# A state space step whose heads, convolution ends and gated norm run as one stream beside the projections

## The chip, the cores and the metric

The kernel runs on one core of a Trainium2 chip. The metric is the device time of one launch in microseconds (us). Before the change the median of 3 runs is 1757.48 us (1754.95 to 1759.02).

## What is computed

Two blocks, one after the other, on 272 rows (16 meta tokens and a sequence of 256) of width 1024, all in float32. The first block is a two-layer model of feed-forward nets, a short convolution and an attention. The second is one mixer layer and a gated convolutional feed-forward net. The change is in the mixer, cut here to what it touches:

```
z, xbc, dt_raw, q, k, v, g_ssd, g_att = split_cols(u @ w_in, IN_WIDTHS)
xbc = silu(causal_dwconv(xbc, conv_w, conv_b))            # 4 taps
xs, bm, cm = split_cols(xbc, (2048, 512, 512))
dt = softplus(dt_raw + dt_bias);  a = -exp(a_log)         # 32 heads of 64
# per head h of group g (8 heads in a group), over chunks of the sequence
cs = cumsum(dt * a)
y  = (C_g B_g^T * exp(cs_t - cs_s), t >= s) @ (x * dt)    # ssd_chunked
y  = y + d_skip * x
g  = y * silu(z)                                          # gated norm
gg = g * rsqrt(mean(g * g over 512 channels) + EPS) * w
merged = sigmoid(g_ssd) * (gg @ w_ssd_branch) + sigmoid(g_att) * (att @ w_attn_branch)
```

The kernel takes the 272 positions at once, in three pieces of 128, 128 and 16, so a head's matrix exp(cs_t - cs_s) is held as 272 + 144 + 16 columns; the last piece (16 rows by 16 columns) is called the corner below.

## The kernel before

**Weights.** Every projection is a sum of products of float32 numbers split in two parts. A weight unit of 1 MB is loaded by SP into one of `raw` buffers (2048 columns, handled in four pieces of 512). ACT writes the high part `wh` of a piece (L1137), then DVE, or POOL for the pieces that the plan names, the low part `wl` (L1626, L1947), and TensorE (PE) takes three products: `XH,wh` and `XL,wh` (L803) and `XH,wl` (L805). With K = 1024 a group of 256 output channels is one unit and 48 matmuls, 24 into each of two PSUM banks; dt, with 32 channels, is 24 matmuls into one. There are `NR` = 4 buffers `raw`, and `NH` = 3 each of `wh` and `wl`; SP loads unit n + 4 once the low part of unit n is written.

**Side steps.** Everything that is no projection is written as a generator on each engine (`pe_steps`, `act_steps`, `dve_steps`, `pool_steps`). All four have the same steps in the same order, some of them empty. A planner (`P`) puts a slot for a step between the matmuls of the groups: `P.rate` is a measure of work per slot, `P.queue(n)` lets n more steps go, `P.credit` holds them back at first, and `P.drain(name)` puts all that are queued before the next group. A step stands at the same slot on every engine, and an engine runs its own instructions strictly in order.

**The mixer's order** is: kv2, q2_0 to 3, z_0 to 7, ga, ya (with the attention's steps beside them), dt, bc_0 to 3 (channels of B and C), xs_0 to 7 (256 channels of x, four heads, each), gs_0 to 3, ys (the branch out of the gated norm).

**Steps of the state space part.** Behind dt come softplus, cumulative sum (DVE, `CSB`, L1415), its transposes (PE L703) and high and low parts `CSH`, `CSL`. `conv4` takes each bc or xs group: a bias and scale out of PSUM on ACT (L1191), three taps for two blocks on DVE (L1684), tanh on ACT (L1197) and its product on DVE (L1689), which ends in `BC` or in one of two buffers `CY`. Four `CB` steps (PE L712, DVE `CBM` L1562) give the products of B and C. For each block c of 128 channels (heads 2c and 2c + 1) there is a T step (PE transposes x, L727; DVE multiplies by dt, `XDT`, L1575), two E steps (PE spreads cs over the partitions, L738; DVE subtracts, L1587, L1588 and for the corner L1590; ACT takes the exponential `EX`; POOL multiplies by `CBM`, L1911, and the corner, L1912) and a y step (PE L643 to L645 into one half of bank 7 for each head; DVE adds the skip into `YB`, L1617; POOL multiplies by silu(z), L1939). The four steps of the gated norm, one for each 512 channels, stand behind all that, beside gs: square on ACT (L1097), sum with a matrix of means on PE (L752), rstd with ln and exp on ACT (L923, L925), product on DVE (L1602), high and low parts `YH` (L1111) and `YL` (L1608).

**The skip's constants.** POOL issues the three small loads `DTB`, `AN`, `DC2` behind ya. Far ahead of them, behind the norm that precedes kv2, it issues the attention's four `B<-strips` loads.

## Time and profile before

| | |
|---|---|
| median of 3 runs | 1757.48 us |
| the profiled execution | 1753.09 us, span 1751.3 us |
| PE busy | 1667.7 us (95%) |
| DVE, ACT, POOL busy | 59%, 52%, 12% |
| mean granted clock of TensorE | 0.986 of 2.4 GHz |
| chain that ended last | PE 84%, issue 4%, ACT 4%, DVE 3%, POOL 3% |
| HBM | 262.89 MB read, 151 GB/s over the span |

The profile is of one execution. Its matmuls are the program's records; a matmul busy for 0.29 us overlaps its neighbour, so the step from one start to the next (about 0.12 us for 258 or 272 columns) is what a matmul takes of the time. "x2" in a row means two records that the view has put together.

### The profile page before, as it was taken

The numbers are of one execution on the slowest core, as the hardware profiler recorded it, in microseconds if no ns is written. First come the engines' busy times: TensorE is split into PE (matmuls) and PEld (weight loads), VectorE is DVE, ScalarE is ACT, GpSimd is POOL, SyncE is SP. The second block draws the span as 40 slices with busy tenths as digits, with TensorE's granted clock in tenths as the row PEclk, the third lists the DMA queues.
The fourth block names the chain that finished last, engine by engine and source line by source line (L and its number), as shares of the span: only waits on it lengthen the run. The fifth ranks groups of instructions, "written<-read, shape, count | busy, mean of one in ns | idle before, by whom it ended". The sixth has DMA issues, their size and how long they took to land.

```text
span 1751.3 us, 31633 instructions
## 1 busy us (share of the span) xinstructions
PE 1667.7 (95%) x12915; PEld 1596.3 (91%) x12915; DVE 1033.4 (59%) x2139; ACT 911.5 (52%) x2008; POOL 217.5 (12%) x257
## 2 busy tenths in 40 slices
...
GB/s 276 175 169 175 182 125 172 122 190 169 177 178 131 169 179 180 194 131 114 121 144 190 177 187 120 176 113 104 113 154 60 78 69 136 201 145 177 179 181 43
DMA packets 260207, 266.00 MB, mean 152 GB/s; under 512 B 4755, under 2 KB 259025, under 8 KB 260064
## 3 DMA queue, kind: packets, MB, share of 16 engines
...
q0 software_dynamic: 1536, 3.28, 0.8%
...
HBM read 262.89 MB, written 1.09 MB: 151 GB/s over the span
## 4 chain that ended last, share of the span: by engine, by line
PE 84%; issue 4%; ACT 4%; DVE 3%; POOL 3%; DMA 0%; SPq 0%; DVEq 0%; POOLq 0%; ACTq 0%
PE ps L803 51%; PE ps L805 25%; POOL EX L1911 2%; PE ps L516 1%; ACT wh L1137 1%; PE ps L772 1%; POOL YB L1939 1%; PE ps L615 1%; POOL EX L1912 0%; ACT H L918 0%; DVE BC L1684 0%; DVE wl L1626 0%; POOL wl L1947 0%; ACT XH L913 0%; PE ps L752 0%
## 5 line engine op out<-in xcount | busy, mean ns | idle before, releaser
L1626 DVE TENSOR_TENSOR wl<-raw,wh 128x512 fp32r<-128x512 f32 x923 | 609.9, 713 | 395.2 <-ACT wh L1137 386.7
L1137 ACT ACTIVATE wh<-raw 128x512 fp32r<-128x512 f32 (+1 forms) x989 | 548.2, 620 | 213.7 <-PE ps L803 212.9
L803 PE MATMUL ps<-XH,wh 128*128 128x272 f32 (+2 forms) x2264 | 577.5, 291 | 16.0 <-ACT XH L913 6.7
L805 PE MATMUL ps<-XH,wl 128*128 128x272 f32 (+2 forms) x2264 | 568.9, 287 | 0.0
L803 PEld LDWEIGHTS ps<-XH,wh 128*128 128x128 f32 x2264 | 431.2, 190 | 21.6 <-issue 14.7
L805 PEld LDWEIGHTS ps<-XH,wl 128*128 128x128 f32 x2264 | 432.5, 191 | 0.2
L803 PE MATMUL ps<-XL,wh 128*128 128x272 f32 (+2 forms) x2264 | 310.6, 288 | 0.2 <-DVE XL L1407 0.2
L803 PEld LDWEIGHTS ps<-XL,wh 128*128 128x128 f32 x2264 | 290.0, 189 | 4.2 <-DVE XL L1407 2.8
L803 PE MATMUL ps<-HH,wh 128*128 128x272 f32 (+1 forms) x704 | 173.1, 284 | 0.0
L805 PE MATMUL ps<-HH,wl 128*128 128x272 f32 (+1 forms) x704 | 173.1, 284 | 0.0
L803 PEld LDWEIGHTS ps<-HH,wh 128*128 128x128 f32 x704 | 132.5, 188 | 0.0
L805 PEld LDWEIGHTS ps<-HH,wl 128*128 128x128 f32 x704 | 132.4, 188 | 0.0
L803 PE MATMUL ps<-KXH,wh 128*128 128x256 f32 (+1 forms) x480 | 121.2, 291 | 2.3 <-ACT KXH L913 2.3
L805 PE MATMUL ps<-KXH,wl 128*128 128x256 f32 (+1 forms) x480 | 118.0, 284 | 0.0
L1947 POOL TENSOR_TENSOR wl<-raw,wh 128x512 fp32r<-128x512 f32 (+1 forms) x66 | 88.1, 1339 | 178.2 <-ACT wh L1137 178.1
L1177 ACT ACTIVATE HH<-SG 128x272 fp32r<-128x272 f32 (+1 forms) x88 | 33.7, 425 | 146.9 <-DVE SG L1643 146.9
L803 PEld LDWEIGHTS ps<-KXH,wh 128*128 128x128 f32 x480 | 91.3, 190 | 7.0 <-issue 5.4
L803 PE MATMUL ps<-HL,wh 128*128 128x272 f32 (+1 forms) x704 | 93.6, 284 | 0.0
L805 PEld LDWEIGHTS ps<-KXH,wl 128*128 128x128 f32 x480 | 91.5, 191 | 0.1
L803 PEld LDWEIGHTS ps<-HL,wh 128*128 128x128 f32 x704 | 89.0, 188 | 0.0
L1172 ACT ACTIVATE SG<-ps 128x272 f32<-128x272 f32 (+1 forms) x88 | 29.6, 388 | 104.8 <-PE ps L803 104.7
L1643 DVE SCALAR_TENSOR_TENSOR SG<-SG,ps 128x272 f32<-128x272 f32 (+1 forms) x88 | 33.8, 425 | 80.0 <-PE ps L803 80.0
...
## 6 DMA issues: line engine op xcount, KB each, us to landing
...
```

The costliest lines, as they stand in the source:

```text
L516: e.matmul(var, mean1[:], SQ[:, k % 4, n0:T], start=k == 0, stop=k == 7).then_inc(s_var, 1)
L615: e.matmul(oo[:, 0:T], VN[:, 0, gs], sw.PT0[:], start=True, stop=False)
L772: mm = e.matmul(PS[6][:, 0:T - n0], mean1[:], SQ2[:, k % 4, 0:T - n0], start=k == 0, stop=k == KD - 1)
L803: mm = e.matmul(o, hi[:, k, c], xk, start=u.first and part == 0 and k == 0, stop=u.last and end)
L805: e.matmul(o, lo[:, k, c], xk, start=False, stop=False)
L1137: e.activation(wh[u.n % NH][:, c], raw[u.n % NR][:, c], ACT.Copy).then_inc(s_hi, 1)
L1172: e.activation(sg[:, m, n0:T], PS[G.b0 + m][:, 0:T - n0], ACT.Silu).then_inc(s_sg, 1)
L1177: e.activation(HH[f][:, 2 * j + m, n0:T], sg[:, m, n0:T], ACT.Copy).then_inc(s_hh, 1)
L1626: e.tensor_tensor(wl[u.n % NH][:, c], raw[u.n % NR][:, c], wh[u.n % NH][:, c].bitcast(F32), ALU.subtract).then_inc(s_lo, 1)
L1643: e.scalar_tensor_tensor(out=sg[:, m, n0:T], in0=sg[:, m, n0:T], scalar=0.5, in1=PS[G.b0 + m][:, 0:T - n0], op0=ALU.mult, op1=ALU.mult).th ...
L1911: e.tensor_tensor(E[:, 0:416], E[:, 0:416], CBM[:, g, 0:416], ALU.mult)
L1947: e.tensor_tensor(wl[u.n % NH][:, c], raw[u.n % NR][:, c], wh[u.n % NH][:, c].bitcast(F32), ALU.subtract).then_inc(s_lop, 1)
```

## The change

1. **Buffers.** `NR, NH, LA` go from 4, 3, 2 to 6, 4, 3. `wl` has as many buffers as `raw` and lies over it: the low part is written in place. SP loads unit n + 6 once PE is done with unit n.
2. **dt first.** The group dt stands right behind kv2, with its side steps (softplus to `CSL`) beside q2. The loads of `DTB`, `AN`, `DC2` stand right behind `B<-strips` on POOL, and ACT waits for them (`s_d`) behind kv2.
3. **Corners of all 32 heads at once**: DVE builds `BD` (32 x 512), PE multiplies it with a part of `tri` into bank 7, DVE adds, ACT takes relu and exp, POOL multiplies by `CBM`. The 16x16 instructions of each head go.
4. **Ends of convolutions** (tanh and product) are side steps, `act_conv_end` and `dve_conv_end`, one group later than the taps; `CY` has four buffers. Odd heads are subtracted on ACT (relu out of PSUM, twice, then exp with scale -1), even heads as before.
5. **y step:** the two heads' matmuls alternate, and both heads are waited for first.
6. **Gated norm in the stream:** after y of blocks 3, 7, 11 and 15 come five steps of the norm of these four blocks (`act_gn`, `dve_gn`, `pe_gn`). DVE adds pairs of squares, so PE has two matmuls in place of four. One buffer `SY` in place of two. The table of ln and exp is no longer loaded ahead of gs.
7. **Plan:** bc is followed by its ends; in the xs stage nothing is drained behind a group (only the `CB` steps behind xs_0), so the T, E and y steps lie beside the groups that follow, and the last of them beside gs.

```diff
-    NR, NH, LA = 4, 3, 2
-    raw = [sb(ctx, f"raw{i}", [128, 2048]) for i in range(NR)]
+    NR, NH, LA = 6, 4, 3
+    with ExitStack() as st:
+        raw = [sb(st, f"raw{i}", [128, 2048]) for i in range(NR)]
+    wl = [sb(ctx, f"wl{i}", [128, 2048], F32R) for i in range(NR)]
...
+    P.group("dt", W_IN, KD, DT0, 1, [(s_sp2, 1)], queue=19)
+    P.rate = 6
...
-    P.group("dt", W_IN, KD, DT0, 1, [(s_sp2, 1)], queue=17)
-    P.rate = 5
     for j in range(4):
-        P.group(("bc", j), W_IN, KD, X_0 + 2048 + 256 * j, 2, two(s_ctap, 6 * j + 4))
-    P.queue(4)
-    P.credit, P.rate, P.pool = -4.0, 26, (2,)
+        P.group(("bc", j), W_IN, KD, X_0 + 2048 + 256 * j, 2, two(s_ctap, 6 * j + 4), queue=1)
+    P.queue(5)
+
+    def ssd_steps(c):
+        return 3 + (c > 1) + 5 * (c > 1 and (c - 2) % 4 == 3)
+    P.credit, P.rate, P.pool = -1.0, 8, (2,)
     for j in range(8):
         P.group(("xs", j), W_IN, KD, X_0 + 256 * j, 2, two(s_ctap, 6 * (4 + j) + 4))
-        P.drain(("xs", j))
-        P.credit = -8.0
-        P.queue(10 + 2 * (j > 0))
-    P.queue(2)
-    P.drain("ssd")
-    P.queue(28)
-    P.rate = 8
+        if j == 0:
+            P.drain("cb")
+            P.credit, P.rate = -4.0, 11.5
+        P.queue(1 + ssd_steps(2 * j) + ssd_steps(2 * j + 1))
+    P.queue(7)
...
+        e.wait_ge(s_em, 2 * c + 2)
+        for n, (rows_, x0, x1) in enumerate(((128, 0, 272), (128, 272, 416), (16, 0, 16))):
+            for par in range(2):
+                h = 2 * c + par
+                M = EX[h % 4][:, x0:x1] if n < 2 else EX2[:, 16 * h:16 * h + 16]
+                mm = e.matmul(PS[7][64 * par:64 * par + 64, T - (x1 - x0):T],
+                              XDT[c % 2][0:rows_, n, 64 * par:64 * par + 64], M, start=n == 0, stop=n == 2)
+                if n == 2:
+                    mm.then_inc(s_y, 1)
+
+    def pe_gn(e, g):
+
+        yield
+        e.wait_ge(s_gadd, g + 1)
+        e.wait_ge(s_xd, min(16, 4 * g + 5))
+        e.matmul(PS[6][:, 0:NV], mean5[:], SY[:, 0, :], start=True, stop=False)
+        e.matmul(PS[6][:, 0:NV], mean5[:], SY[:, 1, :], start=False, stop=True).then_inc(s_gsum, 1)
+        yield
+        yield from idle(3)
...
+        e.wait_ge(s_bd, 1)
+        e.wait_ge(s_c, 32)
+        e.matmul(PS[7][0:16, :], tri[0:32, 128:144], BD[:], start=True, stop=True).then_inc(s_b2, 1)
...
                 yield
-            if c:
+                if (c - 2) % 4 == 3:
+                    yield from pe_gn(e, (c - 2) // 4)
...
+            lo = wl[u.n % NR][:, 0:size].rearrange("p (k c) -> p k c", k=u.g)
...
+    def act_conv_end(e, q):
+        dst = [BC[:, 2 * q + m, :] for m in range(2)] if q < 4 else [CY[(q - 4) % 4][:, m, :] for m in range(2)]
+        if q > 1:
+            e.wait_ge(s_cz, 2 * (q - 2) + 2)
+        for m in range(2):
+            e.wait_ge(s_ctap, 6 * q + 4 + m + 1)
+            e.activation(TH[q % 2][:, m, :], dst[m], ACT.Tanh, scale=0.5).then_inc(s_th, 1)
+    def act_gn(e, g):
+        e.wait_ge(s_yz, 4 * g + 4)
+        if g:
+            e.wait_ge(s_gsum, g)
+        e.activation(SY[:], YB[:, 4 * g:4 * g + 4, :], ACT.Square).then_inc(s_gsq, 1)
+        yield
+        yield
+        e.wait_ge(s_gsum, g + 1)
+        if g:
+            e.wait_ge(s_gn, g)
+        act_rstd(e, PS[6][:, 0:NV], 1, NV, 7 + g)
+        yield
+        e.wait_ge(s_gn, g + 1)
+        for k0 in (4 * g, 4 * g + 2):
+            for k in (k0, k0 + 1):
+                e.activation(YH[:, k, :], YB[:, k, :], ACT.Copy, scale=pc("ssd_norm_w_2", k)).then_inc(s_yh, 1)
+            yield
...
+        e.activation(EX2[:], EX2[:], ACT.Relu, scale=-1.0).then_inc(s_r2, 1)
+        e.wait_ge(s_r2, 1)
+        e.activation(EX2[:], EX2[:], ACT.Exp, scale=-1.0).then_inc(s_x2, 1)
...
+                if h % 2:
+                    e.wait_ge(s_eb, h + 1)
+                    if h > 3:
+                        e.wait_ge(s_y, h - 3)
+                    e.activation(E[:, 0:272], PS[b][:, 0:T], ACT.Relu, scale=-1.0, bias=PCT[:, 0, h:h + 1])
+                    e.activation(E[:, 272:416], PS[b][:, 128:T], ACT.Relu, scale=-1.0,
+                                 bias=PCT[:, 1, h:h + 1]).then_inc(s_er, 1)
+                    e.wait_ge(s_er, h // 2 + 1)
+                    e.activation(E[:], E[:], ACT.Exp, scale=-1.0).then_inc(s_ee, 1)
+                else:
+                    e.wait_ge(s_e, h // 2 + 1)
+                    e.activation(E[:], E[:], ACT.Exp).then_inc(s_ee, 1)
...
+        e.wait_ge(s_d, 48)
+        for a in range(2):
+            pp = slice(64 * a, 64 * a + 64)
+            e.activation(DC[pp, :], DC2[pp, :].rearrange("p (c a) -> p c a", a=2)[:, :, a], ACT.Copy,
+                         scale=0.5).then_inc(s_dc, 1)
+        b0, G = group("dt")
+        e.wait_ge(s_acc, G.acc + 1)
+        e.activation(ZD[:], b0[0:32, 0:T], ACT.Identity, bias=DTB[:, 0:1]).then_inc(s_sp2, 1)
+        side.run(G.after)
...
-        side.run(at["ssd"])
-        e.preload_act_table_set("natural_log_exp_and_others")
...
+        e.tensor_tensor(BD[:].rearrange("p (h t) -> p h t", h=32), DC_[0:32, 256:T].unsqueeze(1).to_broadcast([32, 32, 16]),
+                        ident[0:32, 0:32].unsqueeze(2).to_broadcast([32, 32, 16]), ALU.mult).then_inc(s_bd, 1)
...
-                e.tensor_scalar(E[0:16, 416:432], PS[b][0:16, 256:T], NCT[0:16, 2, h:h + 1], 0.0, ALU.add,
-                                ALU.min).then_inc(s_e, 1)
...
+    def dve_gn(e, g):
+        e.wait_ge(s_gsq, g + 1)
+        e.tensor_tensor(SY[:, 0:2, :], SY[:, 0:2, :], SY[:, 2:4, :], ALU.add).then_inc(s_gadd, 1)
+        yield
+        yield
+        e.wait_ge(s_rs, 8 + g)
+        s = slice(4 * g, 4 * g + 4)
+        e.tensor_tensor(YB[:, s, :], YB[:, s, :], RS[:, 0:NV].unsqueeze(1).to_broadcast([128, 4, NV]),
+                        ALU.mult).then_inc(s_gn, 1)
+        yield
+        for k0 in (4 * g, 4 * g + 2):
+            for k in (k0, k0 + 1):
                 e.wait_ge(s_yh, k + 1)
                 e.scalar_tensor_tensor(out=YL[:, k, :], in0=YB[:, k, :], scalar=pc("ssd_norm_w_2", k),
                                        in1=YH[:, k, :].bitcast(F32), op0=ALU.mult, op1=ALU.subtract).then_inc(s_yl, 1)
-                yield
-        yield from idle(4 + 2 * KD)
+            yield
...
-                e.tensor_tensor(E[:, 0:416], E[:, 0:416], CBM[:, g, 0:416], ALU.mult)
-                e.tensor_tensor(E[0:16, 416:432], E[0:16, 416:432], CBM[0:16, g, 416:432], ALU.mult).then_inc(s_em, 1)
+                e.wait_ge(s_ee, h + 1)
+                e.tensor_tensor(E[:], E[:], CBM[:, g, 0:416], ALU.mult).then_inc(s_em, 1)
...
+        dd = A["ssd_d_2"]
+        e.dma_start(DTB[:], A["ssd_dt_bias_2"].rearrange("l p -> p l")).then_inc(s_d, 16)
+        e.dma_start(AN[:], A["ssd_a_log_2"].rearrange("l p -> p l")).then_inc(s_d, 16)
+        e.dma_start(DC2[:], bass.AP(tensor=dd.tensor, offset=dd.offset, ap=[[0, 128], [1, 32]])).then_inc(s_d, 16)
         group("kv2")
+        group("dt")
...
-                for where, count in dict(units[u.n - NR].lo).items():
-                    e.wait_ge(s_lop if where == "pool" else s_lo, count)
+                which, count = units[u.n - NR].done
+                e.wait_ge(s_acc if which == "acc" else s_unit, count)
```

Three places in the instruction order. First PE at the y step of block 3 (the fourth of 16). Before, PE's rows there, between matmuls of the group xs_3 (`XH,wh` and `XH,wl`), with the transpose of the next block (`ident,CY`) behind:

```order
L643 MATMUL ps<-EX,XDT 64x272
L644 MATMUL ps<-EX,XDT 64x144
L645 MATMUL ps<-EX,XDT 64x16
L643 MATMUL ps<-EX,XDT 64x272
L644 MATMUL ps<-EX,XDT 64x144
L645 MATMUL ps<-EX,XDT 64x16
L727 MATMUL ps<-ident,CY 128x128 x2
L727 MATMUL ps<-ident,CY 16x128
```

Now the same step (`E` is the all-heads corner), with the sum of the first gated norm behind it:

```order
L660 MATMUL ps<-EX,XDT 64x272 x2
L660 MATMUL ps<-EX,XDT 64x144 x2
L660 MATMUL ps<-E,XDT 64x16 x2
L834 MATMUL ps<-XH,wh 128x272
L836 MATMUL ps<-XH,wl 128x272
L834 MATMUL ps<-XH,wh 128x272
L836 MATMUL ps<-XH,wl 128x272
L834 MATMUL ps<-XL,wh 128x272 x2
L670 MATMUL ps<-SY,mean 128x258
L671 MATMUL ps<-SY,mean 128x258
```

The halves alternate, and the sum over four blocks stands ten matmuls' slots behind the step, before the next transposes.

Second ACT at the norm of the first four blocks. Before, behind the last exponential of the whole stage:

```order
L1326 ACT_TABLE_LOAD
L1137 ACTIVATE wh<-raw 128x512 [waits acc,raw1]
L1137 ACTIVATE wh<-raw 128x512 x3
L1161 ACTIVATE GS<-ps 128x258 [waits acc] x2
L1137 ACTIVATE wh<-raw 128x512 [waits acc,raw2]
L1097 ACTIVATE SY<-YB 128x1032 [waits yz]
L1137 ACTIVATE wh<-raw 128x512
L1097 ACTIVATE SY<-YB 128x1032 [waits yz]
L1137 ACTIVATE wh<-raw 128x512
L923 ACTIVATE LNV<-ps,cc 128x258 [waits gsum]
L925 ACTIVATE RS<-LNV 128x258 [waits lnv]
```

Now, beside xs_3 and xs_4 (L1199 is the high part, L1253 the convolution's bias, L1171 an even head's exponential):

```order
L1068 ACTIVATE SY<-YB 128x1032 [waits yz]
L1199 ACTIVATE wh<-raw 128x512
L953 ACT_TABLE_LOAD
L953 ACTIVATE LNV<-ps,cc 128x258 [waits gsum]
L955 ACT_TABLE_LOAD
L955 ACTIVATE RS<-LNV 128x258 [waits lnv]
L1079 ACTIVATE YH<-YB,PV 128x258 [waits gn]
L1079 ACTIVATE YH<-YB,PV 128x258 x3
L1253 ACTIVATE CY<-ps,PV 128x272 [waits acc] x2
L1199 ACTIVATE wh<-raw 128x512 [waits acc,raw4]
L1171 ACTIVATE EX<-EX 128x416 [waits e]
```

The norm stands ahead of the next group's bias and the next heads' exponentials, and there are two table loads in each of the four norms.

Third DVE at the same norm, now (L1766 taps, L1708 low part, L1649 `XDT`; before, its parts stood beside gs):

```order
L1699 SCALAR_TENSOR_TENSOR YB<-CY,DC,ps 128x258 [waits y]
L1680 TENSOR_TENSOR SY<-SY 128x516 [waits gsq]
L1708 TENSOR_TENSOR wl<-raw,wh 128x512 [waits w_hi]
L1685 TENSOR_TENSOR YB<-YB,RS 128x1032 [waits rs]
L1691 SCALAR_TENSOR_TENSOR YL<-YB,PV,YH 128x258 [waits yh] x4
L1766 SCALAR_TENSOR_TENSOR CY<-ps,PV,CY 128x271 [waits cv] x2
L1766 SCALAR_TENSOR_TENSOR CY<-ps,PV,CY 128x270 [waits ctap] x2
L1766 SCALAR_TENSOR_TENSOR CY<-ps,PV,CY 128x269 [waits ctap] x2
L1708 TENSOR_TENSOR wl<-raw,wh 128x512 [waits w_hi]
L1649 TENSOR_TENSOR XDT<-ps,DTT 128x256 [waits y,xt2]
```

The taps of the next group and `XDT` of the next block stand behind the norm's product.

## Rows read from the trace of the kernel before

**Rows 1.** Windows: stretch, length, busy PE, PEld, DVE, ACT, POOL, PEclk, DMA, GB/s.

```profile
1272.20:1333.47 61.27, 45.26 (x317) 42.95 (x315) 39.38 (x80) 27.28 (x59) 13.94 (x12) 0.89 0.39 121
1333.47:1440.20 106.73, 94.32 (x627) 76.76 (x628) 87.55 (x223) 50.53 (x125) 61.88 (x87) 0.97 0.23 70
1375.13:1388.49 13.36, 12.38 (x86) 10.30 (x87) 11.38 (x30) 6.41 (x17) 8.00 (x11) 1.00 0.27 81
1344.40:1347.20 2.80, 0.01 (x1) 0.01 (x1) 2.65 (x8) 1.03 (x3) 0.00 (x0) 0.88 0.68 189
1347.20:1349.70 2.50, 2.48 (x11) 2.42 (x12) 2.43 (x7) 1.31 (x3) 0.44 (x1) 0.50 0.59 208
```

**Rows 2.** PE's waits, 1050 to 1480 us: total, times, longest.

```profile
PE ps L727 <- DVE CY L1689: 12.5, 8, 3.5
PE ps L703 <- DVE CSB L1415: 6.8, 1, 6.8
PE ps L712 <- DVE CBM L1562: 4.6, 2, 3.8
```

**Rows 3.** Timeline of PE: start, length, what, [idle before, releaser].

```profile
1104.12 0.50 PE L693 MATMUL ps<-ident,VV 128*16 128x128 f32 x3 [0.46 <-DVE VV L1797]
...
1275.21 0.29 PE L803 MATMUL ps<-XH,wh 128*128 128x272 f32 x1
...
1333.47 0.52 PE L727 MATMUL ps<-ident,CY 128*128 128x128 f32 x3 [1.34 <-DVE CY L1689]
...
1363.79 0.67 PE L643 MATMUL ps<-EX,XDT 128*64 128x272 f32 x2
...
1365.91 0.39 PE L803 MATMUL ps<-XH,wh 128*128 128x272 f32 x1
...
1467.12 1.91 PE L752 MATMUL ps<-SY,mean 128*128 128x258 f32 x8
...
1469.33 0.28 PE L803 MATMUL ps<-YH,wh 128*128 128x258 f32 x1
```

**Rows 4.** Timeline of DVE, in xs_2 and xs_3 and in gs_3.

```profile
1374.54 0.79 DVE L1689 SCALAR_TENSOR_TENSOR CY<-TH,CY 128x272 f32<-128x272 f32 x2 [0.15 <-ACT TH L1197]
...
1376.62 0.48 DVE L1617 SCALAR_TENSOR_TENSOR YB<-CY,DC,ps 128x258 f32<-128x258 f32 x1
...
1383.77 1.54 DVE L1626 TENSOR_TENSOR wl<-raw,wh 128x512 fp32r<-128x512 f32 x1 [1.10 <-ACT wh L1137]
...
1385.23 2.51 DVE L1684 SCALAR_TENSOR_TENSOR CY<-ps,PV,CY 128x271 f32<-128x271 f32 x6
...
1462.39 0.69 DVE L1626 TENSOR_TENSOR wl<-raw,wh 128x512 fp32r<-128x512 f32 x1
...
1470.93 1.23 DVE L1602 TENSOR_TENSOR YB<-YB,RS 128x1032 f32<-128x1032 f32 x1 [1.61 <-ACT RS L925]
```

**Rows 5.** Timeline of ACT, at the end of the stage and in gs.

```profile
1436.52 1.28 ACT L1326 ACT_TABLE_LOAD   x1
1437.82 2.19 ACT L1137 ACTIVATE wh<-raw 128x512 fp32r<-128x512 f32 x4
...
1446.25 1.07 ACT L1097 ACTIVATE SY<-YB 128x1032 f32<-128x1032 f32 x1
...
1449.45 0.48 ACT L923 ACTIVATE LNV<-ps,cc 128x258 f32<-128x258 f32 x1
...
1472.19 1.72 ACT L1111 ACTIVATE YH<-YB,PV 128x258 fp32r<-128x258 f32 x4 [1.30 <-DVE YB L1602]
```

**Rows 6.** Timeline of POOL: an issue before kv2, a product in xs_2.

```profile
1103.85 0.58 POOL L2011 DMA_DIRECT2D B<-strips  x1
...
1377.17 0.73 POOL L1939 TENSOR_TENSOR YB<-YB,ZS 128x258 f32<-128x258 f32 x1 [5.15 <-DVE YB L1617]
```

**Rows 7.** DMA issues: KB each, median us from issue to landing.

```profile
B<-strips POOLq DMA_DIRECT2D x1, 16.0 KB, 14.2
...
DC<-in_ssd_d POOLq DMA_DIRECT2D x1, 16.0 KB, 3.1
```

More of the change, by code:

```diff
@@ L695, in pe_steps @@
         yield
-        for h in range(19):
-            yield from pe_swa(e, h)
-        yield from idle(16)
         yield from idle(3 + 3 + 9 + 1)
@@ L740, in pe_steps @@
                 yield
-            yield from idle(2)
         for c in (14, 15):
@@ L1307, in scalar @@
         side.run(at["ya"])
-        e.wait_ge(s_d, 48)
-        for a in range(2):
-            pp = slice(64 * a, 64 * a + 64)
-            e.activation(DC[pp, :], DC2[pp, :].rearrange("p (c a) -> p c a", a=2)[:, :, a], ACT.Copy,
-                         scale=0.5).then_inc(s_dc, 1)
-        b0, G = group("dt")
-        e.wait_ge(s_acc, G.acc + 1)
-        e.activation(ZD[:], b0[0:32, 0:T], ACT.Identity, bias=DTB[:, 0:1]).then_inc(s_sp2, 1)
         e.preload_act_table_set("natural_log_exp_and_others")
-        side.run(G.after)
         for j in range(4):
@@ L1536, in dve_steps @@
         yield
-        for h in range(19):
-            yield from dve_swa(e, h)
-        yield from idle(16)
         yield from idle(3)
@@ L1798, in vector @@
         side.run(G.after)
+        side.run(group("dt").after)
         for j in range(4):
```

279 lines of the change are left out of this document (142 added, 137 removed).

## The prediction

> **What bounds the kernel now.** I read the page first. PE is busy 95% of the span and has most of the chain that ended last, so only two things pay here: PE's own time and the stretches in which it stands. Both are in the windows. From the first matmul of dt (1272.20, where the first window starts) to the first of ys (1469.33) are 197.1 us [rows 1, 3]. In the first stretch PE is busy 45.26 of 61.27 us, in the second 94.32 of 106.73 [rows 1]: 16.0 + 12.4 = 28.4 us idle. The waits name most of it: the transposes of x wait 12.5 us for the convolution's end `CY`, one transpose waits 6.8 us for the cumulative sum, two CB steps 4.6 us for `CBM` [rows 2]. The clock adds a little: after PE stood for 2.80 us, the next 2.50 us show a granted clock of 0.50, that is 1.2 GHz [rows 1], in which work takes double, so 1.25 us are lost. In one xs group PE is busy 12.38 of 13.36 us and DVE 11.38 [rows 1]. So the whole idle time in xs is about 1 us a group, and DVE is hardly less full than PE: the stage can't become much faster without less work on both.
>
> **A matmul's step.** bc_0 starts at 1275.21 [rows 3], 3.01 us after dt, whose 24 matmuls take 0.125 each. With 258 columns I take 0.119 (0.125 x 258/272). A y step is 1365.91 - 1363.79 = 2.12 us [rows 3]. What is left of an xs group's 12.38 is 12.38 - 48 x 0.125 - 2 x 2.12 = 2.14 for two T and four E steps, 0.36 each.
>
> **Moved ahead of the stage.** dt (3.0), its transposes (0.65, estimated as six small matmuls of the T kind), the corners' matmul (0.87: 512 columns, four passes, estimated from y's 272 columns in 0.5 us) and a short wait for them (0.7): 5.2 us in kv2 and q2. The 6.8 us wait for the cumulative sum goes: the chain has three groups of q2 to hide in.
>
> **The wait for the skip's constants.** DTB, AN, DC2 are now issued by POOL right behind `B<-strips`, whose last issue ends at 1103.85 + 0.58 and lands 14.2 us after it began, at 1118.05 [rows 6, 7]; DC took 3.1 us in its old place [rows 7]. ACT waits for them behind kv2, and behind that wait are the four high parts of the next weights (2.2 us, the row of 2.19 [rows 5]) and dt's own end ZD, whose PSUM pair q2_1 needs. PE would come to q2_1 at 1104.1 + 3.0 + 6.0 = 1113.1 [rows 3]. If the small loads queue behind the large ones they land near 1117.5, ZD is there 3.3 us later (0.45 + 2.2 + 0.46 + hops), and PE stands 1120.8 - 1113.1 = 7.7 us, with 1.3 for the clock 9.0. If they take 3.1 us (1108.5) it is nothing. The nearest row is that of B on the same queue, 0.6 us before; I take 9.0.
>
> **Start to the first T step.** bc, xs_0 and 28 matmuls of xs_1 are 268 x 0.125 = 33.5. Four CB steps take 1.0 each, their waits fall from 4.6 to 1.8 since the products are two slots apart, and the first T still waits about as long as its row, 1.34 [rows 3]: 40.7 us in place of 61.3.
>
> **T of block 0 to y of block 3.** 96 matmuls (12.0), 12 T and E steps (4.3) and four y steps. Here is the term I am least sure of. The two heads of a block go into two halves of 64 columns of the array, and now alternate. Before, the second head's first matmul came a full 1.06 us after the first's [rows 3], so nothing shows whether two halves can run at once. Bounds: 2.12 (not at all) and 1.06 (fully); I take 1.15, since disjoint columns hold different weights and go to different partitions. Together 20.9, and 2.6 of waits that the shorter y no longer covers, as the way of a block (T, `XDT`, E, exp, two products on POOL) is as long as it was: 23.5. With y at 2.12 it is 24.8 + 0.6 = 25.4.
>
> The Trainium skill (TensorEngine Tiling (Array Packing), Key Properties) says that different tiles execute their loads and matmuls in parallel; by it y comes to 1.06 to 1.15, while the only row we have, of heads one after the other, shows 2.12 and can't contradict it.
>
> **The norm in the stream.** It stands between y of block 3 and T of block 6, and ACT and DVE go through it in order while the next group's bias, taps and `XDT` are behind it. From y's start: y and `YB` 2.2 + 0.48, POOL's product 0.73 [rows 6], square 1.07 and ln 0.48 [rows 5], the pair sum 0.65 (half of 1.23), PE's sum 0.86, table load 1.28 [rows 5] (of two, the first lies in the wait for the sum), exp 0.42, product 1.23 [rows 4], `YH` 1.72 [rows 5], then bias 0.5, taps 2.51, a low part 0.69, `XDT` and even head 1.2, exp 0.46, `wh` 0.55, odd head's relu 0.75, exp 0.46, tanh 0.43 and the first end 0.43 (half of 0.79 [rows 4]): 19.05, with 0.8 for the hops 19.85. PE has 14.0 to do until then: y 2.1, 44 matmuls 5.5, y of block 4 2.1, five T and E steps 1.8, two matmuls of the sum 0.24 and a wait of 2.3 for it. It stands 5.9 us more at T of block 6. From there to y of block 7 are 52 matmuls 6.5, three y 6.4, eight T and E 2.9: 15.7. One cycle of two groups is then 35.5 us (before 26.7, twice 13.36); with overlapping halves 32.7. It comes twice, then a third time from y 11 to the end of the last norm: 88 matmuls 10.6, five y 10.6, T and E 3.2, waits 8.3, and 5.4 for the last square and sum: 38.1, or 34 with overlap. 124 matmuls up to ys are 14.8; the norm's own stretch beside gs (1.55 a sum [rows 3], 1467.12 to 1468.67) is in these.
>
> The Trainium skill (ScalarE: Activation LUTs, What ACT_TABLE_LOAD costs) gives 2.66 us for a switch, load and drain; the row has 1.28, and the next instruction starts 1.30 after it, so the measurement decides. By the page each norm in the chain would be 1.4 us longer, about 4 in all, and the forecast 1757. The same page (Table sets) has one set with both ln and exp, of which this change makes no use.
>
> **Priced at nothing.** Buffers: SP's wait moves from the low part to PE's end of a unit, but six buffers are two more, and the loads are in time everywhere in these stretches (PE's waits name no `raw`). Corners: 32 small instructions less on DVE (about 0.14 each), ACT and POOL are in the groups' shares above; they lie on the way to y, but so do the norm's. Relu of odd heads on ACT (0.75) for 0.69 on DVE: in the chain above.
>
> **Sum.** 40.7 + 23.5 + 2 x 32.7 + 34 + 14.8 = 178.4, plus 5.2 and 9.0: 192.6 against 197.1, so -4.5. The profiled execution's own time, 1753.1, would become 1748.6; the median shown is 4.4 above it, so 1753.
>
> **Rivals.**
> *The constants land early:* no stall before q2_1, -13.5, **1744**. For: they are 16 KB and less. Against: all queues were full then.
> *The chains hide:* if ACT and DVE run ahead, or T waits for less than I think, the 5.9 and 2.3 us in each norm vanish (3 x 8.2 = 24.6), partly with the stall: **1728**. For: DVE is 11.38 of 13.36 before and has 32 corners and half the heads less. Against: the norm's own chain is serial.
> *The halves don't overlap* (the other side): y stays 2.12, the sum is 40.7 + 25.4 + 71 + 38.1 + 14.8 + 14.2 = 204.2, +7.1, **1765**. It decides from y of about 1.5 us (no change) and 1.8 (slower by 0.2%). For: the alternation changes 64 columns' place at each of four passes, and no row shows two at once. With the constants early as well it is -1.9: **1756**, no change.
> *Low parts are slower in the stream:* DVE's 0.69 is 1.54 [rows 4] when POOL works beside it; six such pieces in each of 2.6 norm cycles are 13 us more: **1766**. For: POOL's products fill the stream. Against: the same holds before, where most pieces are short.
> *It does nothing:* the idle 28.4 us only change names. That is the sum of no case by itself; it is in the -4.5 within its error.
>
> **Chances.** Forecast 0.31; constants early 0.18; chains hidden 0.14; no overlap 0.20; no overlap with constants early 0.08; slower low parts 0.09. Out of these: by 0.2% (3.5 us, about what a measurement of this kernel can tell from none) faster 0.50 (0.17 of the forecast's, 0.18, 0.14 and a little), same 0.19 (0.11 of the forecast's and 0.08), slower 0.31 (0.20, 0.09, 0.02). The range 1729 to 1769 leaves out half of the hidden chains (0.07) and the tail of the two slow cases (0.10). The forecast's own is 1747 to 1759.
>
> **What would show it.** In the changed profile: a wait of PE before q2_1 of some 8 us (late constants); a y step of 1.1 to 1.2 us from its first matmul to the next weight product, or 2.1; PE's waits for `CSB` gone; waits of 2 us for the sum of squares and 6 us at T 6, T 10 and T 14 for `CY` or the exponentials; xs groups of 11.7 us without a norm and 16 with one. I am wrong if the waits in the norm cycles are under 2 us (then it is near 1728) or if DVE has work waiting everywhere (then above 1765).

## The result, and the profile after

The changed kernel takes 1780.88 us (median of 4 runs, 1779.46 to 1783.02) where the kernel before took 1756.67: a ratio of 1.0153, 95% interval [1.0136, 1.0170]. That is 24 us slower, outside the forecast's range and the other way. The profiled execution has a span of 1779.6 us, 28.3 more than before.

The windows of the changed kernel, one row for each term of the forecast's sum (stretch, length, busy PE, PEld, DVE, ACT, POOL, PEclk, DMA share, GB/s):

```profile
1095.69:1292.29 196.60, 182.76 (x1331) 163.49 (x1332) 98.05 (x290) 120.34 (x351) 86.90 (x94) 0.97 0.42 125
1292.29:1334.09 41.80, 38.56 (x294) 36.84 (x292) 32.82 (x66) 22.55 (x44) 11.39 (x8) 1.00 0.49 152
1334.09:1365.78 31.69, 25.54 (x168) 23.11 (x168) 19.34 (x46) 15.05 (x33) 12.32 (x13) 0.78 0.22 68
1365.78:1402.94 37.16, 26.19 (x177) 22.57 (x176) 22.63 (x48) 19.85 (x40) 13.57 (x14) 0.86 0.19 57
1402.94:1441.16 38.22, 25.66 (x177) 22.21 (x176) 22.44 (x49) 20.82 (x41) 13.91 (x14) 0.87 0.18 55
1441.16:1482.44 41.28, 26.21 (x178) 22.13 (x178) 19.50 (x39) 22.47 (x42) 16.27 (x16) 0.82 0.17 52
1482.44:1498.53 16.09, 16.09 (x126) 15.99 (x125) 9.06 (x12) 9.80 (x20) 2.71 (x2) 0.93 0.41 131
1292.29:1498.53 206.24, 158.25 (x1114) 142.85 (x1113) 125.80 (x257) 110.53 (x219) 70.16 (x66) 0.88 0.27 82
```

The boundaries are the first matmul of kv2, of bc_0, the T step of block 0, the y steps of blocks 3, 7 and 11, the end of the last norm's sum, and the first matmul of ys. They answer to [rows 1]. From bc_0 to ys the kernel before took 1469.33 - 1275.21 = 194.1 us [rows 3] and the changed one 206.2, of which PE is idle 206.24 - 158.25 = 48.0. In the stretches with the stream the granted clock is 0.78 to 0.87, where the second row of [rows 1] has 0.97.

PE's waits in the changed kernel (total, times, longest), against [rows 2]:

```profile
PE ps L767 <- DVE CY L1675: 30.5, 8, 6.9
PE ps L670 <- DVE SY L1680: 13.9, 4, 4.5
PE ps L834 <- ACT ZD L1348: 8.6, 1, 8.6
PE ps L745 <- DVE CBM L1630: 1.3, 2, 1.2
```

The wait for the cumulative sum (6.8) is gone and that for `CBM` is small. In their place stand 18.0 us more at the T steps for the convolutions' ends, 13.9 for the norm's squares, and 8.6 for the dt group.

PE's timeline, from the y step of block 3, over the sum of the first norm, to the T step of block 6:

```profile
1365.78 0.93 PE L660 MATMUL ps<-EX,XDT 128*64 128x272 f32 x8
...
1366.85 0.39 PE L834 MATMUL ps<-XH,wh 128*128 128x272 f32 x1
...
1371.34 0.70 PE L670 MATMUL ps<-SY,mean 128*128 128x258 f32 x2 [3.47 <-DVE SY L1680]
...
1386.75 0.90 PE L767 MATMUL ps<-ident,CY 128*128 128x128 f32 x3 [5.84 <-DVE CY L1675]
```

The y step is 1366.85 - 1365.78 = 1.07 us, half of [rows 3]'s 2.12: the two heads' matmuls, in two halves of the array, run at once. The wait of 5.84 us at block 6 is the one the forecast worked out (5.9); at blocks 10 and 14, where it expected the same, it is 6.38 and 6.86. After such a wait the clock is down:

```profile
1386.70:1391.20 4.50, 4.45 (x19) 4.13 (x19) 2.13 (x6) 1.31 (x3) 2.68 (x3) 0.50 0.00 2
1347.40:1351.80 4.40, 4.34 (x20) 4.12 (x20) 2.65 (x8) 1.27 (x4) 1.34 (x2) 0.52 0.01 2
```

These are the stretches behind two waits of PE (5.84 and 4.16 us): 4.4 to 4.5 us at 1.2 GHz each, so each of these two costs about 2.2 us more than it lasts. Behind the wait of 2.00 us at block 4 the granted clock is 0.52 for 3.5 us (1361.7 to 1365.2), behind the one of 1.66 us at block 8 it is 1.00.

The late constants: from the view of DMA issues, and ACT's timeline (the bracket is the wait):

```profile
DC<-in_ssd_d POOLq DMA_DIRECT2D x1, 16.0 KB, 12.7
```

```profile
1119.45 0.45 ACT L1344 ACTIVATE DC<-DC 64x16 f32<-64x16 f32 x2 [14.45 <-DMA DC<-in_ssd_d]
1119.93 1.67 ACT L1199 ACTIVATE wh<-raw 128x512 fp32r<-128x512 f32 x3
...
1122.59 0.46 ACT L1348 ACTIVATE ZD<-ps,DTB 32x272 f32<-32x272 f32 x1
```

16 KB that took 3.1 us from issue to landing [rows 7] now take 12.7, behind `B<-strips`. In e1 below, where they are issued ahead of it, they take 3.3.

### The profile page after: what moved, and what is told of

The parts are those of the page before. It is cut to its first block and busy times, and to the rows that moved or that the text cites. A ratio compares the mean times of both kernels' runs of the same rounds, so it can differ in the third digit from the quotient of the medians.

```text
span 1779.6 us, 31457 instructions
## 1 busy us (share of the span) xinstructions
PE 1665.9 (94%) x12901; PEld 1597.4 (90%) x12901; DVE 1021.5 (57%) x2083; ACT 931.1 (52%) x2018; POOL 211.3 (12%) x224
## 5 line engine op out<-in xcount | busy, mean ns | idle before, releaser
L1708 DVE TENSOR_TENSOR wl<-raw,wh 128x512 fp32r<-128x512 f32 x925 | 608.4, 711 | 392.4 <-ACT wh L1199 384.8
L1199 ACT ACTIVATE wh<-raw 128x512 fp32r<-128x512 f32 (+1 forms) x989 | 550.2, 621 | 213.0 <-PE ps L834 212.2
L834 PE MATMUL ps<-XH,wh 128*128 128x272 f32 (+2 forms) x2264 | 584.1, 293 | 21.4 <-ACT ZD L1348 8.6
L834 PEld LDWEIGHTS ps<-XH,wh 128*128 128x128 f32 x2264 | 435.6, 192 | 27.1 <-issue 14.7
L836 PEld LDWEIGHTS ps<-XH,wl 128*128 128x128 f32 x2264 | 436.9, 193 | 0.2
L834 PE MATMUL ps<-XL,wh 128*128 128x272 f32 (+2 forms) x2264 | 319.1, 290 | 0.3 <-DVE XL L1463 0.3
L834 PEld LDWEIGHTS ps<-XL,wh 128*128 128x128 f32 x2264 | 294.8, 191 | 7.0 <-DVE XL L1463 4.2
L2032 POOL TENSOR_TENSOR wl<-raw,wh 128x512 fp32r<-128x512 f32 x64 | 86.1, 1350 | 158.9 <-ACT wh L1199 158.9
```

The costliest lines, as they stand in the source:

```text
L834: mm = e.matmul(o, hi[:, k, c], xk, start=u.first and part == 0 and k == 0, stop=u.last and end)
L836: e.matmul(o, lo[:, k, c], xk, start=False, stop=False)
L1199: e.activation(wh[u.n % NH][:, c], raw[u.n % NR][:, c], ACT.Copy).then_inc(s_hi, 1)
L1708: e.tensor_tensor(wl[u.n % NR][:, c], raw[u.n % NR][:, c], wh[u.n % NH][:, c].bitcast(F32), ALU.subtract).then_inc(s_lo, 1)
L2032: e.tensor_tensor(wl[u.n % NR][:, c], raw[u.n % NR][:, c], wh[u.n % NH][:, c].bitcast(F32), ALU.subtract).then_inc(s_lop, 1)
```

## The experiments

Theory after the first profile: PE waits because every step is asked for too soon behind the step that feeds it (ends of convolutions, norm, constants), and each wait also halves the clock. The first rival: the norm in the stream alone is to blame. The second: ACT and DVE are simply full. All ratios are to the kernel before on the same chip; differences between kernels are those of the ratios times 1755 us. Each kernel ran in 3 rounds, the last six in 5.

| kernel | median us | ratio, 95% interval |
|---|---|---|
| e1 constants first | 1773.96 | 1.0110 [1.0088, 1.0131] |
| e2 alternating halves in the kernel before | 1756.18 | 1.0015 [1.0003, 1.0027] |
| e3 norm behind the stream | 1770.31 | 1.0092 [1.0073, 1.0112] |
| e4 five more slots of lag | 1781.04 | 1.0153 [1.0135, 1.0172] |
| e5 = e1, ends a block earlier | 1765.28 | 1.0061 [1.0046, 1.0076] |
| e6 = e1, no low parts on POOL | 1769.43 | 1.0081 [1.0065, 1.0098] |
| e7 = e1, both heads on DVE | 1780.34 | 1.0147 [1.0130, 1.0164] |
| e8 = e1, one table ahead of ln | 1772.79 | 1.0099 [1.0080, 1.0119] |
| e9 = e5, norm in pieces | 1756.77 | 1.0017 [1.0007, 1.0027] |
| e10 = e9 and three more edits | 1755.86 | 1.0015 [1.0003, 1.0027] |
| e11 = e10, one head after the other | 1759.46 | 1.0028 [1.0018, 1.0038] |
| e12 buffers alone in the kernel before | 1753.50 | 0.9991 [0.9982, 1.0001] |
| e13 changed work in the order of before | 1759.06 | 1.0031 [1.0016, 1.0046] |
| e14 = e13, no low parts on POOL | 1756.03 | 1.0017 [1.0001, 1.0032] |
| e15 = e13, one head after the other | 1761.30 | 1.0038 [1.0023, 1.0053] |
| e17 = e10, ACT's steps a slot later | 1745.12 | 0.9957 [0.9940, 0.9974] |
| e18 = e14, ACT's steps a slot later | 1748.04 | 0.9964 [0.9949, 0.9979] |
| e20 = e17, ACT's steps two slots later | 1754.11 | 0.9994 [0.9979, 1.0009] |

### The constants (e1)

```diff
         e.wait_ge(s_b, 64)
+        e.dma_start(DTB[:], ...)
+        e.dma_start(AN[:], ...)
+        e.dma_start(DC2[:], ...)
         e.dma_start(SNK[:], ...)
         e.dma_start(B2[:, :, 0:256], ...)
...
-        e.dma_start(DTB[:], ...)
-        e.dma_start(AN[:], ...)
-        e.dma_start(DC2[:], ...)
         group("kv2")
```

> The changed kernel with one edit: POOL issues DTB, AN and DC2 ahead of the attention's loads and not behind them. Theory 'late constants': PE's 8.6 us wait for ZD goes, and the half clock behind it (1.5 us): 10 us less than the changed kernel, 1771. Rival 'the queue only moves the wait': weights or B<-strips land later by as much and PE waits for them, or the time won is given back in the stage: within 3 us of 1781.

Expected were 10 us less than the changed kernel, measured 7.5. PE's waits in e1:

```profile
PE ps L767 <- DVE CY L1675: 31.4, 8, 6.7
PE ps L670 <- DVE SY L1680: 12.4, 4, 4.5
...
PE ps L729 <- issue: 3.1, 1, 3.1
```

The row for `ZD` is gone. A part came back as 3.1 us at dt's transposes (L729): with dt no longer held up, PE reaches them before the cumulative sum is done, which the forecast had called hidden. This wait differs between profiles and goes against the one for `VV` before it: e13 has 0.4 us for `VV` and then 3.9 at dt's transposes, e14, the same program up to there, 2.0 and 0.2. So it is no steady price of e1. The theory holds, short by about that.

### The halves (e2)

> The kernel before with one edit: the y step's matmuls alternate between the two heads. Theory 'halves overlap on any kernel and PE's time counts': 16 x 1.07 = 17 us of PE's work less; DVE is busy 11.4 of 13.4 us in an xs group, so at most 2 us a group come through: 8 to 14 us faster, 1743 to 1749. Rival 'the group's end is the bound': the T steps wait for CY by as much more: within 3 us of 1757.

The edit is the alternation of the changed `pe_ssd_y`, in the kernel before. As that step does, it waits for both heads' products before its first matmul. It is 2.6 us slower, not 8 to 14 faster. PE's waits and a window of 100 us of the xs stage in e2, then the same window of the kernel before:

```profile
PE ps L728 <- DVE CY L1690: 20.7, 8, 4.5
```

```profile
1340.00:1440.00 100.00, 77.62 (x587) 67.89 (x588) 83.28 (x210) 46.98 (x119) 61.13 (x86) 0.90 0.24 75
```

```profile
1340.00:1440.00 100.00, 87.98 (x583) 70.97 (x582) 81.51 (x204) 46.66 (x114) 59.20 (x85) 0.97 0.24 74
```

PE does the same matmuls with 10.4 us less busy time and gains nothing: the wait for `CY` grew from 12.5 [rows 2] to 20.7 us, and the clock fell from 0.97 to 0.90. PE's time was not the bound of this stage; what it saved became a longer wait, and the wait cost clock. A smaller part may be the wait for both heads: PE's waits for POOL's product grew from 0.8 to 3.0 us.

### The norm, and more lag (e3, e4)

```diff
-                if (c - 2) % 4 == 3:
-                    yield from pe_gn(e, (c - 2) // 4)
...
-        yield from pe_gn(e, 3)
+        for g in range(4):
+            yield from pe_gn(e, g)
```

> The changed kernel with the gated norm's steps taken out of the stream and put behind y of block 15, beside gs, as four times five steps; rate 9 in place of 11.5 as nine steps a group are left. Theory 'the norm in the stream is what costs': the 13.9 us of waits for the sum, some 17 us of the 30.5 us of waits for CY and the half clock behind them (8 us) go, beside gs they cost under 10: 1781 - 25 = 1756. Rival 'the ends of convolutions stand too close to their T step': only the sum's waits go, the waits for CY stay at 3 to 4 us a group: 1770 or more.

```diff
-            P.credit, P.rate = -4.0, 11.5
+            P.credit, P.rate = -9.0, 11.5
```

> The changed kernel with one number: the credit behind the CB steps is -9 in place of -4, so every state space step stands about five slots (20 matmuls of the group) later than before, behind the taps of its own group. Theory 'ends too close': in groups without a norm the waits for CY (4.2, 2.0, 1.7, 1.7 us) go and in norm cycles they shrink by about 2.5 each, with their clock: 12 us less, 1769. Rival 'the chain through the norm is the bound': what is won at T is waited for elsewhere, within 4 us of 1781.

e3 gains 10.7 us, e4 nothing. PE's waits in e3:

```profile
PE ps L763 <- DVE CY L1670: 25.3, 8, 4.3
PE ps L670 <- DVE SY L1675: 11.7, 3, 4.7
```

```profile
1391.78 0.55 PE L763 MATMUL ps<-ident,CY 128*128 128x128 f32 x3 [3.58 <-DVE CY L1670]
```

Without any norm beside it, each group but the first two (1.4 and 4.3 us) still waits 3.1 to 3.6 us for its end: the rival of e3 was right, and its time of 1770 too. Shifting the whole stream moves the T step and the end that it waits for together: e4's waits for `CY` are 31.3 us, as before.

### The order of the ends (e5), and three single edits (e6 to e8)

```diff
-            if c % 2 == 0:
-                act_conv_end(e, 4 + c // 2)
+            if c == 0 or c % 2 and c < 15:
+                act_conv_end(e, 4 + (c + 1) // 2)
                 yield
...
-            P.credit, P.rate = -4.0, 11.5
+            P.credit, P.rate = -13.0, 11.5
```

> e1 (constants first) with the ends of convolutions (tanh on ACT, product on DVE) put one block earlier in the order of steps, ahead of the previous block's T, E and E steps and not behind them, and the whole stream nine slots later (credit -13), so that an end still stands 16 matmuls behind its taps. Theory 'the order on ACT': before T the tanh waits in ACT's queue behind the previous block's even exponential, relu and odd exponential, which wait for PE's E steps; taken out of that queue, the waits for CY (31.4 us) fall under 10 and the clock behind them comes back: 1774 - 25 = 1749 or less. Rival 'DVE and POOL are simply full or slow each other': the waits reappear under other names, 1766 or more.

8.6 us less than e1. PE's waits in e5:

```profile
PE ps L670 <- DVE SY L1680: 22.1, 4, 6.9
PE ps L660 <- DVE YB L1699: 6.0, 3, 2.0
PE ps L660 <- POOL EX L1997: 4.2, 4, 2.4
...
PE ps L767 <- DVE CY L1675: 2.7, 1, 2.7
```

The waits for `CY` fall from 31.4 to 2.7 us, as the theory has it; but 9.7 us of them reappear at the norm's squares and 7.7 at the y steps (2.5 for `YB` in e1, 6.0 + 4.2 now), as the rival has it. Both theories are right in part, and the time, 1765.3, lies just under the rival's 1766.

e6 gives the planner's `P.pool = ()` in xs and gs:

> e1 with POOL's share of the low parts in the xs and gs stage taken by DVE (one piece in four of each unit). Theory 'contention': a product of the convolution's end takes 0.40 us alone and 0.7 to 1.3 where POOL works beside it; without POOL's 1.3 us pieces the ends are faster and the waits for CY fall by 1 us each: 5 us less, 1769. Rival 'DVE is the bound': its 0.65 us more per group shows, 5 us more, 1779.

e7 puts the odd heads' subtraction back on DVE:

> e1 with the odd heads' subtraction back on DVE, as the kernel before has it (0.76 us there, one exponential on ACT), and not on ACT (0.75 us of relu, then exp). Theory 'the order on ACT': the tanh behind the odd head starts 0.8 us earlier and DVE's 0.7 lies in a wait: 0 to 6 us less, 1768 to 1774. Rival 'DVE is the bound': 16 x 0.7 = 11 us more, 1785.

e8 has one line more in `act_gn`, `e.preload_act_table_set("natural_log_exp_and_others")` ahead of the ln:

> e1 with the table that holds both ln and exp loaded ahead of each norm's ln: the load between ln and exp (1.28 us) leaves the chain and the second one stands at the next tanh. Theory 'the norm's chain is waited for': rstd comes 1.3 us sooner in three norms, but the tanh's load is 1.28 us in the chain to T unless ACT is idle there: 0 to 4 us less, 1770 to 1774. Rival 'table loads lie in waits': no change within 2 us.

e6 is 5 us below e1, e7 6.5 us above it, e8 2 us below it; the intervals of e6 and e8 overlap that of e1, that of e7 only touches it. So only e7 says something: with both heads on DVE the waits for `CY` grow from 31.4 to 40.8 us, and odd heads on ACT are probably worth keeping. e6's theory asked for waits for `CY` shorter by 1 us each; they are 30.5 us in all, 0.9 less, so contention is not shown by it. Nor can an effect of the table load be told. A convolution's end on DVE in the changed kernel, beside a product of POOL:

```profile
1385.60 1.45 DVE L1675 SCALAR_TENSOR_TENSOR CY<-TH,CY 128x272 f32<-128x272 f32 x2 [0.42 <-ACT TH L1061]
```

It takes 1.45 us for two where [rows 4] has 0.79. That POOL's product stretches it is likely, but in no run was the product taken away alone.

### The norm in pieces (e9 to e11)

In e9 the squares stand behind the E steps of the next block, the sum a block later, the product, `YH` and `YL` another block later:

```diff
+            if c > 4 and (c - 5) % 4 < 3:
+                yield from pe_gn(e, (c - 5) // 4, (c - 5) % 4)
```

> e5 (constants first, ends a block earlier) with each norm's steps spread over three blocks: squares behind the E steps of the next block, the sum and rstd a block later, the product and YH, YL another block later; rate 12, credit -15. Theory 'a step that is asked for one slot behind its source is waited for, any step a block behind is free': the 22.1 us of waits for the sum, and the 6 us for YB, fall to under 5 and half of a clock loss of 10 us comes back: 1765 - 25 = 1740. Rival 'ACT and DVE are the bound however the steps are ordered': the waits move to T, E and y steps, 1760 or more.

> e9 with no low parts on POOL in xs and gs, the table of ln and exp loaded ahead of each ln, and the cumulative sum's buffers cleared behind the copy of VV and not ahead of it. The edits alone were worth 5, 2 and at most 3 us: if the chains still bind, 6 to 9 us below e9. Rival 'DVE is the bound once the waits are gone': its 0.65 us more per group makes e10 equal to e9 or up to 5 us slower.

> e10 with the y step's matmuls of one head behind those of the other, as before the change. Theory 'PE's time counts once nothing waits': 16 x 1.07 = 17 us more of PE, at least 10 of them show. Rival 'a shorter y only lengthens a wait': within 4 us of e10, as in the kernel before (+2.6 where 17 us of PE's work left).

e9 gains 7.7 us over e5, where its theory asked for 25 and its rival for none: PE's waits for the sum fall from 22.1 to 1.2 us, but those for `YB` grow from 6.0 to 19.7, and 10.2 for `XDT` are new. e10 gains nothing over e9 (expected were 6 to 9), and e11 is 2.3 us (by the medians 3.6) slower than e10, with overlapping intervals: PE's 17 us are worth 2 or 3 at most. PE's waits in e10:

```profile
PE ps L660 <- DVE YB L1708: 19.6, 9, 5.2
PE ps L669 <- DVE XDT L1653: 6.7, 3, 2.8
PE ps L763 <- ACT LNV L952: 5.2, 3, 1.9
```

The waits have changed names again. Constants (7.5), order of the ends (8.6) and norm in pieces (7.7) add up to 23.8 us: these three are the 24 us by which the change lost. But the stream is then only level with the kernel before. What e10 shows inside stands under "Taking turns".

### Buffers alone, and the order of before (e12 to e15)

> The kernel before with the first part of the change alone: six buffers in place of four, four wh, low parts written in place, SP waiting for PE's end of a unit. Theory 'buffers cost only at the start': PE's first matmul groups come 1 us later, as the changed kernel's norm ahead of kv2 did: 1756 within 2 us of before. Rival 'in-place writing or later loads cost in the dense stages': 4 us or more slower, which would be part of the 24 us.

No difference clear of noise: the buffers explain nothing of the 24 us.

> The changed kernel's work (dt first with the constants ahead, all corners at once, alternating halves, odd heads on ACT, six buffers, pairs of squares) in the order of the kernel before: ends of convolutions right behind the taps, T, E and y steps of a group in a burst inside the next group with everything drained behind it, the norm's four times seven steps beside gs. Theory 'the stream is what costs': the 6.8 us wait for the cumulative sum and its clock go, the group falls from 13.4 to about 12.5 us as DVE has 1.9 us less of work in it: 1755 - 8 - 7 = 1740. Rival 'ACT and DVE bound the stage in any order': a group stays at 13.4 us and the dt group's move is won alone: 1750 or more.

> e13 with DVE taking POOL's piece of each unit in xs and gs. Theory 'contention': POOL's piece delays the odd head's product and stretches DVE's products, 2 to 5 us less than e13. Rival 'DVE is the bound in this order': 0.65 us in each of eight groups, 5 us more.

> e13 with the y step's matmuls of one head behind those of the other. Theory 'a shorter y only lengthens a wait for CY, in the order of before': within 2 us of e13, or faster, as alternating halves cost the kernel before 2.6 us. Rival 'PE's time counts now': 17 us of PE's work back, 4 us or more slower.

e13 takes all of the change's work back into the bursts of the kernel before, and is 0.3% slower than it, as its rival had it (1750 or more), not 1740. One xs group of e13 (from T step to T step) answers to the third row of [rows 1]:

```profile
1381.53:1395.17 13.64, 11.79 (x86) 10.08 (x87) 9.05 (x22) 7.30 (x17) 6.95 (x7) 0.87 0.26 77
```

DVE has 9.05 us of work in place of 11.38, PE 2.1 us less of matmuls (11.79 busy in place of 12.38, since its clock is 0.87 and not 1.00), and yet the group takes 13.64 us in place of 13.36. No engine is full; what the group lost on work came back as waits and clock. (e14 is 2.5 us below e13 and e15 1.2 above it, both within their intervals: POOL's piece and PE's time matter as little here.) So neither the stream's order nor the sum of any one engine's work is the bound; that ACT and DVE are simply full, the second rival, falls here. A bound by the way from one engine to the other is not excluded by it.

### Taking turns (e17, e18, e20)

In e10, ACT's and DVE's timelines around one block:

```profile
1387.06 0.55 ACT L1172 ACTIVATE EX<-EX 128x416 f32<-128x416 f32 x1 [2.22 <-DVE EX L1664]
1387.52 0.47 ACT L1165 ACTIVATE EX<-ps,PCT 128x272 f32<-128x272 f32 x1
...
1388.75 0.62 ACT L1203 ACTIVATE wh<-raw 128x512 fp32r<-128x512 f32 x1
```

```profile
1386.68 0.35 DVE L1664 TENSOR_SCALAR EX<-ps,NCT 128x144 f32<-128x144 f32 x1
1389.40 1.16 DVE L1717 TENSOR_TENSOR wl<-raw,wh 128x512 fp32r<-128x512 f32 x1 [2.37 <-ACT wh L1203]
```

ACT stands 2.2 us for DVE's `EX` of the same slot, with a high part `wh` further back in its queue that it could have done; DVE then stands 2.4 us for that `wh`. The two engines take turns. e17 moves ACT's steps one slot behind DVE's and POOL's two; e18 moves ACT's alone, by one:

```diff
+        yield from idle(1)                # act_steps; idle(2) in pool_steps
         for c in range(16):
```

> e10 (stream in pieces) with ACT's state space steps one slot later than DVE's and PE's, and POOL's two. Theory 'turns in a slot': ACT's exponential no longer waits for the DVE instruction of its own slot, the high part behind it is done meanwhile, and DVE's waits for wh (2.4 us a group) fall: 1756 - 10 = 1746. Rival 'the sum of ACT's and DVE's work along the chain of a block binds': the same waits in other places, within 3 us of 1756.

> e14 (order of before, no low parts on POOL) with ACT's steps for a block's two heads one slot later than DVE's, in a slot that was empty. Theory 'turns in a slot': the wait of 1.9 us before each even head's exponential is partly filled with a high part: 2 to 5 us less than e14's 1756. Rival 'the tail from a group's end to T is the bound' (bias, taps, tanh, product, 4.4 us, of which 20 matmuls cover 2.5): the burst's inside doesn't matter, within 2 us.

10.2 us less than e10, as expected, and 9.3 less than e14, where 2 to 5 were expected; both are faster than the kernel before. DVE's waits in a window of the stage (1340 to 1420 us), first e14, then e18:

```profile
DVE wl L1697 <- ACT wh L1192: 14.2, 6, 2.4
```

```profile
DVE wl L1697 <- ACT wh L1192: 7.3, 6, 1.2
```

PE's for `CY` in the same two kernels:

```profile
PE ps L762 <- DVE CY L1663: 17.0, 8, 4.3
```

```profile
PE ps L762 <- DVE CY L1663: 8.7, 8, 3.1
```

and ACT's for `EX`:

```profile
ACT EX L1162 <- DVE EX L1648: 23.2, 12, 2.8
```

```profile
ACT EX L1162 <- DVE EX L1648: 20.9, 8, 2.8
```

In e18 the first two waits are halved. ACT's own wait for DVE's `EX` is not gone, though: of the two in a group, 2.8 and 1.1 us in e14, the first stays and only the second goes. What changed is what stands behind it: the high part now comes ahead of the second block's odd head and not behind it, so `wl`, the taps and the tanh come earlier. A group (from tanh to tanh) takes 11.85 us in e18 in place of 13.62, with PE busy 10.72 in place of 11.77, as the clock is back at 1.00 from 0.87. In e17 it is less clear: over 1340 to 1440 us ACT's waits for `EX` are 32.6 us where e10 has 35.0, DVE's for `wh` 12.4 where e10 has 15.3, and the largest change is in DVE's wait for the convolution's bias on ACT, 13.0 to 4.6. So the gain of one slot of lag is measured in a stream and in bursts alike; by which wait it comes is seen in e18 only.

The stage by itself, in the profiled executions (first matmul of bc_0, length from there to ys, PE's busy time and clock in it):

| kernel | bc_0 at | bc_0 to ys | PE busy | clock |
|---|---|---|---|---|
| before | 1275.21 | 194.12 | 165.69 | 0.95 |
| changed | 1292.29 | 206.24 | 158.25 | 0.88 |
| e10 | 1288.13 | 188.10 | 151.79 | 0.92 |
| e17 | 1282.62 | 177.97 | 148.91 | 0.94 |
| e14 | 1280.72 | 190.27 | 155.76 | 0.89 |
| e18 | 1285.76 | 182.57 | 153.90 | 0.92 |

In this stretch e10 is already 6.0 us faster than the kernel before and e17 16.1; what stands ahead of it eats a large part. bc_0 starts 5.5 to 12.9 us later even with the constants early (e14, e10). dt's own matmuls are ahead of bc_0 in every kernel, so this is the price of its transposes, the corners, waits and clock, where the forecast had 5.2 - 3.0 = 2.2.

> e17 with ACT's steps two slots behind DVE's and POOL's three, and the stream one slot later (credit -16). If turns in a slot still bind, ACT's waits for EX (33 us in 100) fall again and the time goes to 1740 or less; if what is left are the norm's pieces and YB behind the taps on DVE, it stays within 3 us of 1745, or is slower, as EX and tanh come later for PE.

e20 is 6.5 us slower than e17. DVE's waits for `wh` are nearly gone (12.4 to 1.1 us in 100), but those for the tanh have grown from 5.1 to 16.6. ACT's waits for `EX` did not fall (35.7): neither the time nor the sign that e20 was to show for the theory came. One slot is the best of the three lags (none, one, two).

## Why the prediction was wrong

By its own steps, in the profiled executions:

| term | forecast | measured |
|---|---|---|
| moved ahead, with the constants | 5.2 + 9.0 = 14.2 | 196.60 - 177.80 = 18.8 |
| bc_0 to T of block 0 | 40.7 | 41.8 |
| T of block 0 to y of block 3 | 23.5 | 31.7 |
| y of block 3 to y of block 11 | 65.4 | 37.16 + 38.22 = 75.4 |
| y of block 11 to the last norm's sum | 34 | 41.3 |
| from there to ys | 14.8 | 16.1 |
| sum | 192.6 | 225.0 |

The kernel before, from its first matmul of kv2 to dt, and from bc_0 to ys:

```profile
1094.40:1272.20 177.80, 174.86 (x1299) 156.98 (x1300) 85.75 (x271) 112.22 (x331) 81.09 (x89) 1.00 0.44 130
...
1275.21:1469.33 194.12, 165.69 (x1136) 144.92 (x1135) 144.16 (x324) 97.48 (x223) 81.14 (x100) 0.95 0.28 88
```

**Right:** the y step at 1.07 where I took 1.15, so the rival of halves that don't overlap was wrong. The Trainium skill's rule that different tiles execute their loads and matmuls in parallel (TensorEngine Tiling (Array Packing), Key Properties) agrees with this 1.07. The constants behind `B<-strips` (8.6 us where I had 7.7), the long waits at blocks 6, 10 and 14 (5.84, 6.38 and 6.86 for 5.9), the loss of the wait for the cumulative sum at its old place.

**The step that failed** is "Together 20.9, and 2.6 of waits that the shorter y no longer covers". I priced a stretch without a norm by adding up PE's work and a small remainder. The stage was bound by the way from a group's last matmul over ACT and DVE to the T step, so a shorter y only lengthened a wait (e2 shows that in the kernel before by itself, and in e3, without a norm, each group still waits 3.1 us and more). Measured are 4.16 and 2.00 us of waits in this stretch, 6.2 for 2.6, at the two T steps that need a fresh end, and PE busy 25.54 us for 20.9, as part of the work ran at 1.2 GHz: 31.7 for 23.5. The same kind of wait, at nothing in the forecast, stands at blocks 8 and 12 (1.66 and 1.71 us).

**The clock** was counted once, 1.3 us behind the constants. From bc_0 to ys PE's busy time is 158.25 us. By the kernel before it should be 165.69, less 17 for y and about 1 for the sums, so 147 or 148: some 10 us are extra time of work at 1.2 GHz behind waits. With 48.0 - 30.7 = 17 us more idle than forecast (30.7 is the forecast's 178.4 less 147.7 of work, so by this reckoning only) and 4.6 ahead of the stage, that is the 32 us by which the sum was short. Of the 4.6, 2.5 are waits (8.6 for 7.7 at `ZD`, 1.6 for `VV` where the kernel before has 0.5, 1.2 for 0.7 at the transposes and corners) and 2.1 are PE's busy time, in part clock: behind the wait of 8.6 us it is 0.50 for 2.9 us and more.

**The sum's waits** at the three norms in the stream were 3.5 to 4.5 us, forecast 2.3: the right mechanism, too small.

**A slip in the sum** hid part of the miss. Between T of block 6 and y of block 7 stand two y steps (blocks 5 and 6), not three. By its own terms a cycle is 1.2 to 2.1 us too long for it, and without the slip the forecast would have been some 2 to 4 us further off.

**The sign** that the forecast named for a time above 1765, DVE with work waiting everywhere, is not what came: DVE is busy 125.8 of the 206.2 us. The time went to waits along chains and to the clock behind them.

**What lay under it,** and what I had not seen in the trace of before, although its rows show it. ACT's timeline of the kernel before, in xs_3:

```profile
1378.33 0.55 ACT L1086 ACTIVATE EX<-EX 128x416 f32<-128x416 f32 x1 [1.92 <-DVE EX L1588]
```

ACT stands 1.92 us for DVE there as well. The engines' in-order queues in shared slots make ACT and DVE take turns. e13 shows that the changed work is bound in the order of before as much as in the stream, e17 and e18 that one slot of lag of ACT is worth 9 to 10 us in either. The kernel before itself was not run with such a lag.

**Not settled:** how far the rest could go. In e17 PE still waits 10.8 us for `YB` and 6.0 for `XDT`. Taking a head's steps to yet other slots wasn't tried. e17 moves POOL's steps and ACT's tanh too, and no run separates them. Whether POOL slows DVE is argued from DVE's rows (a product of 0.40 us stretched to 0.7) and not separated from POOL's own delay. Why the wait at dt's transposes is long in some profiles and short in others is open, and no run takes dt's move back by itself.
